# One hybrid decoder layer in float32: attention over memory by products made once from weights and memory

## The chip, the cores and the metric

The kernel runs on one core of a Trainium2 chip. The metric is the device time of one execution in microseconds (us). Of the core's engines PE (TensorE) multiplies matrices, ACT (ScalarE) and DVE (VectorE) do elementwise work, POOL (GpSimd) does elementwise work in SBUF and issues DMAs, and SP issues DMAs.

## What is computed

A prompt of 2048 tokens and 8 single decode tokens, model width 1024, pass through one layer: a mixer (short convolution and mLSTM), attention over 256 memory rows, and a SwiGLU network. The change is in the attention, four heads of width 256:

```python
def mem_kv(mem, g_mem, w_xkv):
    kk, vv = jnp.split(rmsnorm(mem, g_mem) @ w_xkv, 2, axis=-1)
    return kk.reshape(B, M, X_HEADS, X_HEAD_DIM), vv.reshape(B, M, X_HEADS, X_HEAD_DIM)

def cross_attn(xn, mk, mv, w_xq, w_xo):
    q = (xn @ w_xq).reshape(B, T, X_HEADS, X_HEAD_DIM)
    s = jnp.einsum('bthd,bmhd->bhtm', q, mk.astype(q.dtype)).astype(jnp.float32) * (X_HEAD_DIM ** -0.5)
    p = jax.nn.softmax(s, axis=-1).astype(xn.dtype)
    o = jnp.einsum('bhtm,bmhd->bthd', p, mv.astype(xn.dtype)).reshape(B, T, X_HEADS * X_HEAD_DIM)
    return o @ w_xo
```

The prompt has one memory (keys and values from `mem_kv`, both outputs too). Each decode token has its own cached keys and values.

## The kernel before

**Tiling.** Activations lie with features on the partitions and tokens along the rows. The prompt is cut in five blocks of 4, 3, 3, 3 and 3 chunks of 128 tokens (`BLK`). The 8 decode tokens ride as extra columns: in the mixer of block 1 (`DM`), the output and query products of block 2 (`DO`), the attention output and network of block 3 (`DX`).

**Products in three passes.** A float32 product with a weight is made from a rounded high part and a remainder: high by high, high by low, low by high (`gemm`, L518). A weight group is one 128 by 1024 piece (512 KB); a `gemm` of a group is 8 x 3 = 24 matmuls whose moving width is the block's token count (512, 384, or 392 with the decode tokens).

**Weight stream.** The 16 groups of memory weights, then 121 groups per block: gates, sigmoids, four heads of six, output (`O_OUT`, 8), queries (`O_XQ`, 8), attention output (`O_XO`, 8) and network. For the memory groups and block 0, SP loads raw weights into two buffers (`w_raw`, L326), ACT casts the high part into one of `NS` = 5 slots (`w_high`, L823), and DVE (memory groups, L1175) or POOL (block 0, L419) subtracts to get the low part. The subtract frees the raw buffer. In block 0 SP also stores both parts to `split_d` (1 MB); blocks 1 to 4 load them from there, one 1 MB load a group.

**Attention of a block.** Eight query groups with the scores (L682, three-pass, 256 wide), the turning of probabilities (`ptrans`, L692) and the products with the values (`pv`, L699, plain float32) hooked between them; the softmax is `maxima` (DVE, L1439), `exps` (ACT, L1011, 128 by 256 each) and `normalise` (DVE, L1450). Then eight `O_XO` groups.

**Opening.** The kernel makes keys and values of the memory (16 groups, 256 wide), turns the values (L552) and prepares the first block's activations on DVE (L1164, L1170) and ACT (L840).

**Order.** Every engine runs its own program in order, written out by hand; engines meet at semaphores. In `w_high(g)` ACT waits for the raw load of group g + `NS` and for group g to be used up.

**End.** After the last group come the last sum of squares (L526), a root, eight multiplications (L1224), four stores of `y` and three of states.

## Time and profile before

| | |
|---|---|
| runs, median of 3 | 2973.12 us (2971.23 to 2975.67) |
| the profiled execution | 2972.26 us |
| its span, first to last instruction | 2970.5 us |
| PE busy / weight loads | 2921.0 us (98%) / 2759.7 us (93%) |
| DVE / ACT / POOL busy | 1212.2 / 761.0 / 379.7 us |
| moved by DMA | 776.02 MB, 261 GB/s |

The profile is of one execution. A busy engine is one with an instruction in flight; matmuls overlap in their pipeline (a 384-wide one is shown with some 338 ns), so what a matmul costs is read from the chain of waits, whose pieces give a stretch's length and its number of matmuls. A plain float32 product shows as two matmul records.

### The profile page before, as it was taken

How to read it: one execution, taken by the hardware profiler on the slowest of the kernel's cores; microseconds unless marked ns; L12 is line 12 of the kernel's file. 1: busy time of each engine (PE TensorE's matmuls, PEld its weight loads, DVE VectorE, ACT ScalarE, POOL GpSimd, SP SyncE). 2: the span in 40 equal slices, each digit the busy share in tenths (PEclk: the TensorE clock that was granted, in tenths of full speed). 3: DMA queues.
4: the chain of work that ended last, by engine and by line, in shares of the span. 5: the costliest groups of instructions: out<-in, count | busy, mean ns of one | idle time of the engine just before them, and what ended most of it. 6: DMA issues, size and time to landing. Idle time of an engine off the chain costs nothing.

```text
span 2970.5 us, 39232 instructions
## 1 busy us (share of the span) xinstructions
PE 2921.0 (98%) x16162; PEld 2759.7 (93%) x16162; DVE 1212.2 (41%) x2337; ACT 761.0 (26%) x1510; POOL 379.7 (13%) x252
## 2 busy tenths in 40 slices
PE   7899999999999999999999999999999999999998
PEld 6788778888899999999999999999999999999998
DVE  6455554224624444233344546334422243442223
ACT  4443443232332220113232011322311032231001
POOL 0443434444210000000000111000000000000000
PEclk9999999999999999999999999999999999999999
DMA  5876858788876488777667989866467777646675
GB/s 190 321 269 225 282 203 298 277 277 309 300 274 244 162 324 305 264 264 285 219 226 273 338 321 372 308 226 249 174 241 260 260 268 266 229 179 248 254 268 195
DMA packets 126585, 776.02 MB, mean 261 GB/s; under 512 B 14885, under 2 KB 18405, under 8 KB 46665
## 3 DMA queue, kind: packets, MB, share of 16 engines
q1 hardware_dynamic: 109744, 710.71, 66.0%
q0 software_dynamic: 13904, 59.48, 5.8%
q10 hardware_dynamic: 2760, 3.33, 0.4%
q8 instruction: 129, 2.11, 0.3%
q14 instruction: 48, 0.39, 0.0%
HBM read 633.52 MB, written 139.94 MB: 260 GB/s over the span
## 4 chain that ended last, share of the span: by engine, by line
PE 90%; DMA 4%; DVE 2%; ACT 2%; POOL 1%; issue 1%; SPq 0%; DVEq 0%; ACTq 0%
PE gb L518 83%; DMA w_raw<-w_st 2%; PE ta L682 2%; DMA w_hl<-split_d 1%; POOL w_hl L419 1%; PE td L699 1%; PE tb L699 1%; ACT w_hl L823 1%; DMA w_raw<-w_kv 1%; PE ta L603 0%; PE tb L572 0%; DVE w_hl L1175 0%; PE ta L526 0%; PE tb L614 0%; PE td L621 0%
## 5 line engine op out<-in xcount | busy, mean ns | idle before, releaser
L518 PE MATMUL gb<-xn_hi,w_hl 128*128 128x384 f32 (+2 forms) x6440 | 1770.4, 350 | 14.2 <-DVE xn_lo L1170 7.7
L518 PEld LDWEIGHTS gb<-xn_hi,w_hl 128*128 128x128 f32 x6440 | 1178.7, 188 | 73.2 <-DVE xn_lo L1170 8.8
L518 PE MATMUL gb<-xn_lo,w_hl 128*128 128x384 f32 (+2 forms) x3240 | 1123.1, 347 | 0.0
L518 PE MATMUL gb<-act_hi,w_hl 128*128 128x384 f32 (+3 forms) x3296 | 872.4, 344 | 18.4 <-DVE w_hl L1175 10.6
L518 PEld LDWEIGHTS gb<-act_hi,w_hl 128*128 128x128 f32 x3296 | 598.8, 189 | 46.3 <-DVE w_hl L1175 10.9
L518 PEld LDWEIGHTS gb<-xn_lo,w_hl 128*128 128x128 f32 x3240 | 609.5, 188 | 28.7 <-issue 1.2
L518 PE MATMUL gb<-act_lo,w_hl 128*128 128x384 f32 (+3 forms) x1648 | 563.9, 342 | 0.0
L1218 DVE TENSOR_TENSOR work<-gb,r_res 128x384 f32<-128x384 f32 (+2 forms) x260 | 151.8, 585 | 652.0 <-PE gb L518 588.1
L419 POOL TENSOR_TENSOR w_hl<-w_raw,w_hl 128x1024 fp32r<-128x1024 f32 x120 | 292.4, 2440 | 413.7 <-ACT w_hl L823 413.7
L518 PEld LDWEIGHTS gb<-act_lo,w_hl 128*128 128x128 f32 x1648 | 311.6, 189 | 13.6 <-issue 0.7
L1410 DVE TENSOR_TENSOR x<-x,gb 128x384 f32<-128x384 f32 (+2 forms) x200 | 115.4, 581 | 373.2 <-PE gb L518 369.9
L823 ACT ACTIVATE w_hl<-w_raw 128x1024 fp32r<-128x1024 f32 x132 | 138.9, 1057 | 329.6 <-DMA w_raw<-w_st 158.4
L1080 ACT ACTIVATE work<-work 128x384 f32<-128x384 f32 (+2 forms) x110 | 59.9, 545 | 504.1 <-DVE work L1218 504.0
L1083 ACT ACTIVATE act_hi<-work 128x384 fp32r<-128x384 f32 (+2 forms) x110 | 60.1, 546 | 346.2 <-DVE work L1637 346.2
L997 ACT ACTIVATE work<-x 128x384 f32<-128x384 f32 (+2 forms) x120 | 65.6, 546 | 270.0 <-DVE x L1410 249.7
L1420 DVE TENSOR_TENSOR r_res<-r_res,work 128x384 f32<-128x384 f32 (+2 forms) x120 | 94.5, 787 | 68.6 <-ACT work L997 67.2
L1637 DVE TENSOR_TENSOR work<-work 128x384 f32<-128x384 f32 (+2 forms) x110 | 87.4, 794 | 35.2 <-ACT work L1080 24.0
L382 POOL DMA_DIRECT2D big<-rows_d x20 | 10.9, 550 | 675.1 <-DMA rows_d<-big 675.1
L887 ACT ACTIVATE big<-gb,cst 128x384 f32<-128x384 f32 (+1 forms) x80 | 48.5, 607 | 186.6 <-PE gb L518 186.0
L1320 DVE TENSOR_TENSOR work<-ta,big 128x128 f32<-128x128 f32 x64 | 18.7, 292 | 186.8 <-ACT work L968 144.4
L1624 DVE TENSOR_TENSOR act_lo<-work,act_hi 128x384 fp32r<-128x384 f32 (+2 forms) x110 | 85.6, 778 | 12.5 <-ACT act_hi L1083 11.8
L1423 DVE SCALAR_TENSOR_TENSOR xn_lo<-x,cst,xn_hi 128x384 fp32r<-128x384 f32 (+2 forms) x80 | 55.8, 698 | 0.0
(248 smaller groups left out, 1806.9 us busy)
## 6 DMA issues: line engine op xcount, KB each, us to landing
w_hl<-split_d SPq DMA_DIRECT2D x484, 1024.0 KB, 5.2
split_d<-w_hl SPq DMA_DIRECT2D x121, 1024.0 KB, 5.0
w_raw<-w_st SPq DMA_DIRECT2D x121, 512.0 KB, 6.0
w_raw<-w_kv SPq DMA_DIRECT2D x16, 512.0 KB, 3.6
big<-kd_d POOLq DMA_DIRECT2D x8, 1024.0 KB, 9.0
big<-vd_d POOLq DMA_DIRECT2D x8, 1024.0 KB, 11.3
x<-x_blk POOLq DMA_DIRECT2D x8, 768.0 KB, 8.0
big<-x_blk POOLq DMA_DIRECT2D x6, 768.0 KB, 6.0
```

The costliest lines, as they stand in the source:

```text
L419: pool.tensor_tensor(lo_w, raw_w, hi_w.bitcast(F32), ALU.subtract).then_inc(w_lo_done, 1)
L518: mm = pe.matmul(gb[:, ps, 0:wd], a[:, s, k * P:(k + 1) * P], r[:, k, 0:wd], start=(first and k == ks[0] and i == 0), stop=(last and k == ...
L682: mm = pe.matmul(ta[:, t // 2, (t % 2) * 256:(t % 2) * 256 + 256], a[:, kt, t * P:(t + 1) * P], r[:, kt, :], start=(dt == 0 and i == 0), s ...
L823: act.activation(w_hi[:, n % NS, :], w_raw[:, n % NR, :], ACT.Copy).then_inc(w_hi_done, 1)
L997: act.activation(sq_res[:, 0:wd], x[:, e, 0:wd], ACT.Square).then_inc(res_sq, 1)
L1080: act.activation(et[:, 0:W], gt[:, 0:W], ACT.Silu).then_inc(e_ffn, 1)
L1083: act.activation(act_hi[:, f, 0:W], ht[:, 0:W], ACT.Copy).then_inc(hid_hi, 1)
L1218: return lambda ps: v.tensor_tensor(dst[:, 0:wd], ps[:, 0:wd], r_res[:, 0:wd], ALU.mult)
L1410: return lambda ps: v.tensor_tensor(x[:, e, 0:wd], x[:, e, 0:wd], ps[:, 0:wd], ALU.add)
L1420: v.tensor_tensor(acc_res[:, 0:wd], acc_res[:, 0:wd], sq_res[:, 0:wd], ALU.add).then_inc(res_acc, 1)
L1624: v.tensor_tensor(act_lo[:, f, 0:W], ht[:, 0:W], act_hi[:, f, 0:W].bitcast(F32), ALU.subtract).then_inc(hid_lo, 1)
L1637: v.tensor_tensor(ht[:, 0:W], et[:, 0:W], ut[:, 0:W], ALU.mult).then_inc(h_ffn, 1)
```

## The change

Products with two fixed factors are made once: for each head the query weights times the keys (1024 by 256), and the values times the output weights (256 by 1024). Together they are sixteen 128 by 1024 pieces.

- **Opening.** 16 more weight groups follow the memory groups (`w_xq` transposed, `w_xo`), through the same two raw buffers, cast by ACT, subtracted by POOL. From them PE makes 32 banks of product (16 of 12 matmuls 256 wide, 16 of 6 matmuls 512 wide). ACT copies the even banks, DVE the odd; ACT stores all, whole float32, to `made_d` in rows of 1 KB (first 16) and 512 bytes. SP loads them in block 0 as raw weights in the places of queries and attention output. `NS` goes from 5 to 6; the slots take the place of `mem_k_hi`, `mem_k_lo` and `mem_v`.
- **Attention.** `wide(p, ...)` gives the scores of two heads at once: activations are stationary, the made piece moves 512 wide. Two halves, each 24 matmuls for every chunk. Query groups, scores against keys and products with values are gone; the turned probabilities go in three passes straight into `O_XO`. The row sums come as columns (`sum_cols`, one product a chunk).
- **Decode tokens.** Their queries are made apart in block 2 (`decode_queries`, plain float32, 16 products 512 wide, between `O_XO` groups), their attention output in block 3 (`decode_outputs`, 16 such, between `O_OUT` groups, then 8 small turning products). 16 loads of 512 KB on POOL's queue bring the weights.
- **Rows.** In each block three row tiles are now stacked and turned by one product a chunk (12 wide) where there were three (4 wide); their store is two DMAs.
- **Decode pieces.** `PIECE_AT` puts two of them later in block 2's network.
- **End.** The last sum of squares takes its last term as a second product instead of a DVE addition, the table load is earlier, POOL multiplies two of the eight tiles of `y`, and the stores go in the order 0, 2, 6, 4.

```diff
+G_KV = 32
+NPRE = 32
 O_GATE = 0
...
-NS = 5
+NS = 6
...
-PIECE_AT = [2 * f + 1 for f in range(1, 8)] + [16 + m for m in (0, 1, 2, 4, 5, 6)] + [G1 + 2 * f + 1 for f in range(3)]
+PIECE_AT = [2 * f + 1 for f in range(3, 8)] + [16 + m for m in range(8)] + [G1 + 2 * f + 1 for f in range(3)]
...
+def attends(g):
+    return g >= G_KV and O_XQ <= (g - G_KV) % G_BLK < O_FF[0]
...
+                if attends(g):
+                    src = made_d[g - gw(0, O_XQ)]
...
+                    if raws[i] == gw(0, O_XQ):
+                        for slot_stored in pre_stored:
+                            sp.wait_ge(slot_stored, 16 * (NPRE // 8))
...
+            for k in (0, 2, 6, 4):
+                if k == KT - 2:
+                    sp.wait_ge(y_pool, 2)
+                else:
...
+            pool.wait_ge(r_done, r_res_at(NB - 1, 2))
+            for k in (KT - 2, KT - 1):
+                pool.tensor_tensor(x[:, k, 0:W], x[:, k, 0:W], r_res[:, 0:W], ALU.mult).then_inc(y_pool, 1)
...
+            for h in range(HEADS):
+                pe.wait_ge(mem_lo, 2 * h + 2)
+                for j in range(4):
+                    i = h * 4 + j
+                    bank = pre_bank(i)
+                    for n in range(2):
+                        for dt in range(2):
+                            g = G_MEM + 2 * h + dt
+                            if j == 0 and n == 0:
+                                slot_ready(g)
+                            c = (2 * j + n) * P
+                            for f, (a, r) in enumerate([(w_hi, act_hi), (w_hi, act_lo), (w_lo, act_hi)]):
+                                mm = pe.matmul(bank[:, n * NMEM:(n + 1) * NMEM], a[:, g % NS, c:c + P], r[:, 2 * h + dt, NMEM:2 * NMEM],
+                                               start=(dt == 0 and f == 0), stop=(dt == 1 and f == 2))
...
+                for j in range(4):
...
+                    for dt in range(2):
+                        g = G_MEM + KT + 2 * h + dt
+                        if j == 0:
+                            slot_ready(g)
+                        for f, (a, r) in enumerate([(act_hi, w_hi), (act_lo, w_hi), (act_hi, w_lo)]):
+                            mm = pe.matmul(bank, a[:, 2 * h + dt, mt * P:(mt + 1) * P], r[:, g % NS, half * 512:half * 512 + 512],
+                                           start=(dt == 0 and f == 0), stop=(dt == 1 and f == 2))
...
+                def turn_rows():
+                    pe.wait_ge(rows_exp, b + 1)
+                    pick = ident[0:3 * ROWS, 0:3 * ROWS].rearrange("p (i c) -> p i c", c=ROWS)[:, :, 0:HEADS]
                     for c in range(CH):
-                        a = (i * CH + c) * HEADS
-                        mm = pe.matmul(tb[:, a:a + HEADS], row[:, c * P:(c + 1) * P], ident[0:ROWS, 0:HEADS], start=True, stop=True)
...
+                        pe.wait_ge(dw_loaded[i % 4], 16 * ((KT + i) // 4) + 16)
+                        for half, bank in enumerate((ta[:, 1, :], td)):
+                            mm = pe.matmul(bank[0:NDEC, :], dy[:, i * NDEC:(i + 1) * NDEC], dwt[:, i % 4, half * 512:half * 512 + 512],
+                                           start=i == 0, stop=i == KT - 1)
+                        mm.then_inc(dw_used, 1)
...
+                def sum_cols():
+                    pe.wait_ge(res_acc, b * 27 + 9)
                     for t in range(CH):
-                        for dt in range(2):
-                            kt = 2 * h + dt
...
+                def score_bank(p, t):
+                    if p == 0:
+                        return gb[:, (gw(b, O_XQ) + t) % NP, :] if t < NP else gm[:, :]
+                    return (ta[:, 0, :], ta[:, 1, :], td[:, :], tb[:, :])[t]
+                def ptrans(h, mt):
+                    bank = gm if b == 0 and h < 2 else (gm, tb)[mt]
+                    pe.wait_ge(p_done, ch0(b, h // 2 * 2 + 2))
...
+                def wide(p, hooks):
+                    for q in range(4):
+                        g = gw(b, O_XQ) + 4 * p + q
+                        slot_ready(g)
                         for t in range(CH):
-                            m = pe.transpose(bank[:, t * P:(t + 1) * P], prob[:, t, mt * P:(mt + 1) * P], ident)
-                        m.then_inc(pt_done, 1)
-                def pv(h):
-                    pe.wait_ge(pt_evac, (b * HEADS + h) * 2 + 2)
-                    for dt, bank in enumerate((td, tb)):
-                        for mt in range(MT):
-                            mm = pe.matmul(bank[:, 0:TOK], mem_v[:, mt, h * 256 + dt * P:h * 256 + (dt + 1) * P],
-                                           prob_t[:, mt, 0:TOK], start=(mt == 0), stop=(mt == MT - 1))
-                        mm.then_inc(pv_done, 1)
-                opening(gw(b, O_XQ), W, 0)
-                q_hooks = {3: {3: lambda: scores(0)}, 4: {6: lambda: ptrans(0)}, 5: {2: lambda: scores(1) or pv(0)},
-                           6: {6: lambda: ptrans(1) or scores(2)}, 7: {3: lambda: pv(1)}}
-                for m in range(2, KT):
-                    gemm(gw(b, O_XQ + m), W, xn_hi, xn_lo, hooks=q_hooks.get(m))
+                            if q == 0 and p == 0 and t < NP:
+                                read_out(pe, gw(b, O_OUT + KT - NP) + t)
+                            if q == 0 and p == 1 and t == 2:
+                                pe.wait_ge(rcol_done, b + 1)
+                            for n in range(2):
+                                kt = 2 * q + n
+                                if p == 0 and t == 0:
+                                    pe.wait_ge(res_lo, b * 16 + kt + 1)
+                                for f, (a, r) in enumerate([(xn_hi, w_hi), (xn_lo, w_hi), (xn_hi, w_lo)]):
+                                    mm = pe.matmul(score_bank(p, t), a[:, kt, t * P:(t + 1) * P], r[:, g % NS, n * 512:n * 512 + 512],
+                                                   start=(kt == 0 and f == 0), stop=(kt == KT - 1 and f == 2))
+                            if t == CH - 1:
+                                mm.then_inc(group_done, 1)
+                            elif q == 3:
+                                mm.then_inc(s_done, 1)
+                            if (q, t) in hooks:
+                                hooks[q, t]()
+                wide(0, {(1, CH - 1): sum_cols})
+                if b == 0:
+                    wide(1, {(1, 3): lambda: ptrans(0, 0), (2, 1): lambda: ptrans(0, 1), (2, 3): lambda: ptrans(1, 0),
+                             (3, 1): lambda: ptrans(1, 1)})
+                else:
+                    wide(1, {(1, 2): lambda: ptrans(0, 0) or ptrans(0, 1), (2, 2): lambda: ptrans(1, 0) or ptrans(1, 1)})
                 def o_wait(k):
                     pe.wait_ge(o_lo, b * 8 + k + 1)
-                    if b == DX and k == 0:
...
+                def decode_product(i, rows, lhs, bank):
+                    pe.wait_ge(dw_loaded[i % 4], 16 * (i // 4) + 16)
+                    for half in range(2):
+                        mm = pe.matmul(bank[half][0:NDEC, :], lhs, dwt[:, i % 4, half * 512:half * 512 + 512],
+                                       start=rows == 0, stop=rows == KT - 1)
+                    mm.then_inc(dw_used, 1)
...
+            W = w_ffn(NB - 1)
+            pe.wait_ge(res_acc, (NB - 1) * 27 + 26)
+            pe.matmul(ta[:, 0, 0:W], ones, acc_res[:, 0:W], start=True, stop=False)
+            pe.wait_ge(res_sq, NB * 24)
+            pe.matmul(ta[:, 0, 0:W], ones, sq_res[:, 0:W], start=False, stop=True).then_inc(ssq_done, 1)
...
+                pre_left(act, i)
+                h, j = (i // 4) % HEADS, i % 4
+                if i < NPRE // 2:
+                    dst = made_d[4 * (h // 2) + j].rearrange("p (n h m) -> p n h m", n=2, h=2)[:, :, h % 2, :]
+                    src = made[:, i % 8, :].rearrange("p (n m) -> p n m", n=2)
+                else:
+                    kt, m0 = 2 * h + j // 2, KT + j % 2 * 4
+                    dst = made_d[m0:m0 + 4, :, kt * P:(kt + 1) * P].rearrange("m p c -> p m c")
+                    src = made[:, i % 8, :].rearrange("p (m c) -> p m c", m=4)
+                act.dma_start(dst, src).then_inc(pre_stored[i % 8], 16)
+            for i in range(NPRE):
+                if i % 2 == 0:
+                    pre_made(act, i)
+                    after(act, pre_stored[i % 8], 16 * (i // 8))
+                    act.activation(made[:, i % 8, :], gb[:, (G_MEM + i) % NP, :], ACT.Copy).then_inc(pre_a, 1)
+                if i:
+                    store_made(i - 1)
+                if i % 4 == 3:
+                    w_high(G_MEM + i // 4 * 2)
+                    w_high(G_MEM + i // 4 * 2 + 1)
+                if i < KT:
+                    read_out(act, G_MEM - 1)
+                    act.activation(act_hi[:, i, 0:NMEM], vfeat[:, i, :], ACT.Copy).then_inc(mem_hi, 1)
+                elif i < 2 * KT:
+                    next_high(0, i - KT)
+            store_made(NPRE - 1)
...
+                w_high(gw(b, O_XQ))
+                norm_cols(b, r_res_at(b, 0))
+                for q in range(1, 4):
+                    w_high(gw(b, O_XQ + q))
                 exps(0)
-                q_high(3)
-                pt(0)
-                q_high(4)
+                w_high(gw(b, O_XQ + 4))
+                w_high(gw(b, O_XQ + 5))
+                prob_high(0)
+                w_high(gw(b, O_XQ + 6))
+                prob_high(1)
+                w_high(gw(b, O_XQ + 7))
```

ACT at the end of the opening, before: a cast of weights a group, beside casts of activations and keys.

```order
L823 ACTIVATE w_hl<-w_raw 128x1024
L840 ACTIVATE xn_hi<-big 128x512
L873 ACTIVATE mem_k_hi<-x 128x256 x2
L823 ACTIVATE w_hl<-w_raw 128x1024
L873 ACTIVATE mem_k_hi<-x 128x256 x2
L892 ACTIVATE big<-gb,cst 128x512
L823 ACTIVATE w_hl<-w_raw 128x1024
```


ACT after, in the second half of the made products: a copy of a bank, two stores, and after each four banks two casts.

```order
L1083 ACTIVATE big<-gb 128x512
L1077 DMA made_d<-big 128x4x128 x2
L998 ACTIVATE w_hl<-w_raw 128x1024 x2
L1083 ACTIVATE big<-gb 128x512
L1077 DMA made_d<-big 128x4x128 x2
L1083 ACTIVATE big<-gb 128x512
L1077 DMA made_d<-big 128x4x128 x2
L998 ACTIVATE w_hl<-w_raw 128x1024 x2
L1083 ACTIVATE big<-gb 128x512
L1077 DMA made_d<-big 128x4x128 x2
L1083 ACTIVATE big<-gb 128x512
L1077 DMA made_d<-big 128x4x128 x2
L998 ACTIVATE w_hl<-w_raw 128x1024 x2
```


The casts now stand between the copies that free PE's banks. PE in the attention of block 1 before: a query group with two products of values hooked in (`td`, `tb`, 384 wide).

```order
L518 MATMUL gb<-xn_hi,w_hl 128x384 x2
L518 MATMUL gb<-xn_lo,w_hl 128x384
L518 MATMUL gb<-xn_hi,w_hl 128x384
L699 MATMUL td<-big,mem_v 128x384 x2
L699 MATMUL tb<-big,mem_v 128x384 x2
L518 MATMUL gb<-xn_hi,w_hl 128x384
L518 MATMUL gb<-xn_lo,w_hl 128x384
L518 MATMUL gb<-xn_hi,w_hl 128x384 x2
L518 MATMUL gb<-xn_lo,w_hl 128x384
```


PE after in block 1, the second half of the scores: the turning of head 0's probabilities (`gm`, `tb`) between two pieces.

```order
L853 MATMUL td<-w_hl,xn_hi 128x512 x2
L853 MATMUL td<-w_hl,xn_lo 128x512
L853 MATMUL td<-w_hl,xn_hi 128x512
L835 MATMUL gm<-mats,work 128x128 x3
L835 MATMUL tb<-mats,work 128x128 x3
L853 MATMUL ta<-w_hl,xn_hi 128x512
L853 MATMUL ta<-w_hl,xn_lo 128x512
L853 MATMUL ta<-w_hl,xn_hi 128x512 x2
```


The value products have no counterpart. PE in block 2, fifth `O_XO` group, before: one turning of decode queries.

```order
L518 MATMUL gb<-act_hi,w_hl 128x384 x2
L518 MATMUL gb<-act_lo,w_hl 128x384
L518 MATMUL gb<-act_hi,w_hl 128x384
L722 MATMUL tb<-mats,dec 64x128
L518 MATMUL gb<-act_hi,w_hl 128x384
L518 MATMUL gb<-act_lo,w_hl 128x384
```


PE after, in the fourth `O_XO` group: four float32 products for the decode queries (8 rows out, 512 wide); three more such hooks follow.

```order
L613 MATMUL gb<-act_lo,w_hl 128x384
L613 MATMUL gb<-act_hi,w_hl 128x384
L881 MATMUL ta<-dwt,dec 8x512
L881 MATMUL td<-dwt,dec 8x512
L881 MATMUL ta<-dwt,dec 8x512
L881 MATMUL td<-dwt,dec 8x512
L613 MATMUL gb<-act_hi,w_hl 128x384
L613 MATMUL gb<-act_lo,w_hl 128x384
```


One turning is gone, sixteen products have come.

## Rows read from the trace of the kernel before

**Rows 1.** The page, parts 1 and 2: whole kernel.

```profile
PE 2921.0 (98%) x16162; PEld 2759.7 (93%) x16162; DVE 1212.2 (41%) x2337; ACT 761.0 (26%) x1510; POOL 379.7 (13%) x252
...
PEclk9999999999999999999999999999999999999999
```

**Rows 2.** The longest of the waits of PE: us in total, times, longest.

```profile
PE gb L518 <- DVE w_hl L1175: 10.6, 2, 9.4
```

**Rows 3.** Chain of waits, opening of the kernel: start us, us, what.

```profile
26.92 2.88 PE gb L518 x24
...
48.07 3.95 DMA w_raw<-w_kv
...
94.65 5.47 PE gb L518 x24
...
114.45 0.98 PE tb L572 x8
```

**Rows 4.** Chain of waits, attention of block 1.

```profile
985.76 2.15 PE ta L682 x18
...
993.63 0.33 PE gm L692 x3
...
998.54 1.29 PE td L699 x4
...
1015.35 4.16 PE gb L518 x24
```

**Rows 5.** Chain of waits, attention of block 2.

```profile
1553.41 4.22 PE gb L518 x24
```

**Rows 6.** Chain of waits, attention of block 0.

```profile
331.24 4.30 DVE act_lo L1465
...
354.71 1.72 PE td L699 x4
```

**Rows 7.** Groups by form, PE: what, count, busy us, mean ns.

```profile
L682 PE MATMUL ta<-mem_k_hi,act_hi 128*128 128x256 f32 x128 | 37.0, 289 | 1.7 <-DVE act_lo L1465 1.7
...
L699 PE MATMUL td<-big,mem_v 128*128 128x384 f32 x64 | 23.3, 485 | 0.0
```

**Rows 8.** Groups by form, ACT, whole kernel.

```profile
L1011 ACT ACTIVATE work<-ta,work 128x256 f32<-128x256 f32 x64 | 29.5, 469 | 45.6 <-DVE work L1442 45.6
...
L1011 ACT ACTIVATION_READ_ACCUMULATOR work<-ta,work 128x1 f32 x64 | 12.7, 199 | 0.0
```

**Rows 9.** Groups by form, DVE, whole kernel.

```profile
L1450 DVE TENSOR_SCALAR work<-work 128x256 f32<-128x256 f32 x64 | 22.6, 354 | 2.3
...
L1439 DVE TENSOR_REDUCE work<-ta 128x2 f32<-128x512 f32 x24 | 16.6, 691 | 27.8 <-PE ta L682 27.7
```

**Rows 10.** Timeline of ACT, end of the memory stage.

```profile
59.12 1.04 ACT L823 ACTIVATE w_hl<-w_raw 128x1024 fp32r<-128x1024 f32 x1
...
62.65 1.04 ACT L823 ACTIVATE w_hl<-w_raw 128x1024 fp32r<-128x1024 f32 x1
```

**Rows 11.** Timeline of POOL, first subtracts of weights.

```profile
78.44 2.35 POOL L419 TENSOR_TENSOR w_hl<-w_raw,w_hl 128x1024 fp32r<-128x1024 f32 x1 [4.57 <-ACT w_hl L823]
82.15 2.46 POOL L419 TENSOR_TENSOR w_hl<-w_raw,w_hl 128x1024 fp32r<-128x1024 f32 x1 [1.36 <-ACT w_hl L823]
88.05 2.38 POOL L419 TENSOR_TENSOR w_hl<-w_raw,w_hl 128x1024 fp32r<-128x1024 f32 x1 [3.44 <-ACT w_hl L823]
```

**Rows 12.** Timeline of DVE in the same stretch.

```profile
67.13 0.68 DVE L1170 TENSOR_TENSOR xn_lo<-big,xn_hi 128x512 fp32r<-128x512 f32 x1
...
82.33 2.83 DVE L1170 TENSOR_TENSOR xn_lo<-big,xn_hi 128x512 fp32r<-128x512 f32 x1
```

**Rows 13.** The line that loads raw weights: issue to landing, all its loads.

```profile
DMA to landing us min/median/max: 3.1/5.9/11.8
```

**Rows 14.** Chain of waits, last microseconds.

```profile
2959.00 0.57 DVE r_res L1420
...
2962.88 3.17 DVE x L1224 x6
```

572 lines of the change are left out of this document (320 added, 252 removed).

## Prediction

> **What bounds the kernel now.** I read the page first, then the waits of PE, then the chain of waits. PE is busy 98% of the span, and its granted clock stays at the upper level of 2.4 GHz in nearly every slice [rows 1]. The longest of PE's waits sum to 10.6 us, for DVE's weight parts in the opening [rows 2]. From block 1 on the chain is PE, matmul after matmul, and no other engine's work stands in it for long. So a matmul taken away there is worth its spacing, and the opening has to be looked at by itself, since weights and not matmuls set its pace.
>
> The profile shows some 340 ns for one matmul, but they overlap. The cost is a piece of the chain divided by its count: 256 wide 2.88/24 = 0.120 us [rows 3], 384 wide 4.16/24 = 0.173 [rows 4], 392 wide 4.22/24 = 0.176 [rows 5], 512 wide 5.47/24 = 0.228 [rows 3]. A plain float32 product is two records: 384 wide 1.29/2 = 0.645 [rows 4], 512 wide 1.72/2 = 0.86 [rows 6], and a 4-wide turning of a row 0.98/4 = 0.245 [rows 3]. A turning by transpose is 0.33/3 = 0.11 [rows 4].
>
> **PE's work outside the opening.** All of it is on the path.
> - Scores: 24 matmuls a chunk, 16 chunks, 384 x 0.120 = 46.1 us go (a third of them is the first line of [rows 7]).
> - Products with values: 16 a block. 64 x 0.645 + 16 x 0.86 = 55.1 go (the 64 records of `td`, 384 wide, are half of the four narrower blocks [rows 7]).
> - Query groups: 576 x 0.173 + 192 x 0.176 + 192 x 0.228 = 177.2 go; `wide` has 48 matmuls a chunk, 768 x 0.228 = 175.1 come. The columns are the same, only fewer and wider: -2.1.
> - Turning of values, 16 x 0.11: -1.8. Rows: 48 products become 16, 32 x 0.245: -7.8. Eight columns less in `O_XO` of block 3: -0.6.
> - Sums as columns: 17 products of 0.245 for five of some 0.68: +0.8. No row shows one moving column; the 4-wide one is the nearest, and its bounds (nothing to double) are worth 4 us each way.
> - Decode tokens: 32 x 0.86 + 8 x 0.245 = +29.5. No row has a product with 8 rows out; I take the 512-wide price, since its rows with 128 out stream the same columns. The bounds are 0.228 (one pass) and 0.86, so this can be up to 20 us less.
>
> Sum: -46.1 - 55.1 - 2.1 - 1.8 - 7.8 - 0.6 + 0.8 + 29.5 = **-83.2 us**.
>
> Beside the rows on 512-wide matmuls stands a figure of the Trainium skill (TensorE: Matmul & The Clock Gate, "Back-to-back issue gap"): about 131 ns each at 512 columns. By it the scores would come out 768 x 0.097 = 74 us lower still, an estimate. The 24 matmuls of this kernel that took 5.47 us [rows 3] are of the same width and type, so I go by them.
>
> **The opening.** The made products are 192 x 0.120 + 96 x 0.228 = 44.9 us of PE, but their weights come slower. A raw buffer's round is load, cast, subtract. The load is 3.95 in the memory stage [rows 3], with a median of 5.9 over the kernel and up to 11.8 [rows 13]; I take 4.2, near the first, since the stores beside it are 256 KB and not 1 MB. With the cast 1.04 [rows 10], the subtract 2.4 [rows 11] and 0.1 of semaphores it is 7.8 us for one of two buffers, 3.9 a group. The casts of two groups lie 3.5 apart in the memory stage [rows 10], the subtracts beginning at 78.44 and 88.05 are two groups apart, 4.8 each [rows 11]: these are the bounds.
>
> Two things add to 3.9. DVE's operations with two inputs in SBUF stand still beside POOL's subtract: the same one took 0.68 us at 67.13 and 2.83 at 82.33, just as POOL ran 82.15 to 84.61 [rows 11, 12], and in block 0 one of 0.69 took 4.30 [rows 6]. The opening has 24 of these, and they hold POOL likewise. And ACT is in order: after every four banks it casts two groups, six ahead, and while it waits for their load it copies no bank, so PE stops after three. I take 4.4 a group.
>
> The last bank waits for a copy that stands behind the cast of group 35. Group 16's load lands at about 62 (casts of earlier groups at 59.12 and 62.65 [rows 10], one slot more now). 19 groups x 4.4 = 84 brings group 35 to 146; cast 1.1, copy 0.6, last product 1.4, some semaphores: 150. The gate product, 16 x 0.228 = 3.6, ends at 153.5. Before, the piece of 24 at 94.65 [rows 3] holds the last three matmuls of the first sigmoid group (one turning stands after its first 21): that group ended at 95.3 and would have begun, without gaps, at 95.3 - 5.5 - 0.4 = 89.4. So the opening costs **+64 us** with its 44.9 of matmuls; at 3.5 a group +47, at 4.8 +72. Afterwards weights are no nearer to the edge than now: 24 x 0.228 = 5.5 us of PE a group against 4.8.
>
> **Waits in the attention.** In block 1 the first half's softmax has half of the second half, 12 x 3 x 0.228 = 8.2 us, as cover. The second half's last bank is done as the half ends. Then come maximum 0.69 + 0.27, two exponentials with their accumulator reads 2 x (0.47 + 0.20) = 1.34 [rows 8], and reciprocal and two scalings 0.16 + 2 x 0.35 [rows 9]. Behind the two earlier banks that is 4.1 us. PE has four pieces of `O_XO`, 4 x 6 x 0.173 = 4.2. It just fits. In block 0 a cast stands ahead of the exponentials, and four banks take some 7.5 us against 5.5: 2 us. That one replaces some of block 0's stall before the scores, where DVE took 4.30 [rows 6]. The decode weights are loaded 13 us ahead of their use (two groups of 4.2 and three float32 pairs), longer than the longest raw load [rows 13]. I put all new waits less the old ones at **+2 us** (range -3 to +20).
>
> **The end.** An addition of 0.57 leaves the path [rows 14]. DVE multiplies six tiles (3.2 us as the six of [rows 14]) and not eight; POOL's two, by size 0.9 each from its 2.4 a group [rows 11], either run beside them (-1.1) or in turn with them (+0.7), since they have two inputs in SBUF on both sides [rows 12]. **-0.3 us**.
> The Trainium skill (SBUF — State Buffer, "Who interferes with whom") has it that such a pair excludes one another for the whole instruction; by that rule, to which [rows 12] agrees with 2.83 against 0.68, the end would come to +0.1, without it to -1.7.
>
> **Sum.** -83.2 + 64 + 2 - 0.3 = -17.5. From the profiled execution's 2972.26 that is 2954.8; its median of runs lies 0.9 higher, so 2955.6, say **2955 us**.
>
> **Rivals.**
> 1. *The stream is smooth.* Loads keep the memory stage's 3.5 us a group [rows 10], since PE, ACT and DVE have little else: -17. 2938. For it: stores are small. Against: the subtract on POOL is twice as long as DVE's was.
> 2. *The softmax comes late.* If maximum, exponentials and scaling go one after another, three banks take 3 x 3.2 = 9.6 from 2.7 before the half's end, 6.9 against 4.2 of cover, and the second turning waits for its evacuation too: about 4 us a block, 20 in all. 2975, no change. It decides from 4.2 us after the half. For it: only 0.1 us of slack by rows.
> 3. *The stores of made products slow the stream; slower than before.* 32 stores go out in rows of 512 bytes and 1 KB beside the loads. If a load then takes 8.4, inside the 11.8 seen [rows 13], a group takes 6.0, and 19 x 6.0 puts the gate's end at 183: +93. 2985. It decides at 5.5 us a group, a load of 7.3. Against: 4.8 is what 1 MB stores did to it [rows 11].
> 4. *A 512-wide matmul in `wide` is spaced like a 256-wide one.* 768 x (0.228 - 0.120) = 83 less: 2872. Against it stand the 24 in 5.47 [rows 3].
> The Trainium skill's figure, above, points this way and gives 2881 as an estimate.
> 5. *The change does not do what it says*: the columns of queries and of new scores are equal, so if the values' and scores' time had been hidden, nothing is gained. But those pieces stand in the chain itself [rows 4]; I give it nothing of its own.
>
> **Chances.** Forecast (2944 to 2966) 0.58; rival 1 0.14, the cheap decode products with it 0.03; rival 2 0.12; rival 3 0.10; rival 4 0.01; something else 0.02. For 8 in 10 the range goes from 2936, with most of rival 1 in it, to 2972, without rival 3 and the upper part of rival 2. A measurement of this kernel tells a change from none at about 0.2%, 6 us. Faster by more than that is the forecast, rivals 1 and 4 and a quarter of rival 2: 0.80; within it 0.10; slower 0.10.
>
> **What the profile after would show.** The gate product's end near 153, and waits of PE in the opening put down to ACT's copies and POOL's subtracts; casts 4.4 us apart on average from group 16 on. `O_XQ` of block 1 as 144 matmuls in 33 us with no wait inside, and the attention of blocks 1 to 4 each some 19 us shorter (72 x 0.120 + 16 x 0.645 + 0.4). The decode products at 0.86 each. I am wrong if the opening's end is off by more than 10 us, if PE waits before the turning of heads 2 and 3 in every block, or if PE loses time in block 2's network to the later decode pieces.

## Result: slower by 0.4%

The changed kernel takes 2982.5 us (median of 6), the kernel before 2970.9 beside it (median of 6); the ratio is 1.0037, 95% interval 1.0025 to 1.0049. The forecast was 2955, faster. One of the six executions of the changed kernel took 3214 us at a granted clock of 0.85; the ratio leaves it out, and the median of the other five is 2982.1. Its profiled execution took 2980.44 us, with a span of 2978.6.

The page, parts 1 and 4 (chain: share of the span by engine), which answer to [rows 1]:

```profile
PE 2892.0 (97%) x15739; PEld 2706.0 (91%) x15739; DVE 1177.9 (40%) x2240; ACT 754.5 (25%) x1472; POOL 427.9 (14%) x286
...
PE 85%; DMA 6%; DVE 2%; POOL 2%; ACT 2%; issue 2%; SPq 0%; ACTq 0%; DVEq 0%
```

PE's busy time fell by 29 us, and the time still rose: PE stands still more. Where, is seen when the first matmul of each stage is looked up in both traces (us from the start of the span; the last row ends with the execution). "Forecast" is made of the prediction's own terms.

| stage | before | after | change | forecast |
|---|---|---|---|---|
| up to the end of the gate product | 89.4 (without gaps) | 159.7 | +70.3 | +64 |
| block 0, rest of the mixer | 182.1 | 191.6 | +9.5 | -3.8 |
| block 0, mixer's output products | 44.0 | 44.0 | 0 | 0 |
| block 0, attention and `O_XO` | 119.2 | 104.7 | -14.5 | -23.2 |
| block 0, network | 362.0 | 361.8 | -0.2 | 0 |
| blocks 1 to 4 and the end | 2175.6 | 2118.7 | -57.0 | -54.5 |

From block 1 on all came as forecast and 2.5 us better. Everything that is missing, 28 us, is missing before block 1 begins: at 861.8 instead of 796.6 us, +65 where +37 was forecast.

The longest waits of PE in the first 505 us (us in total, times, longest), which answer to [rows 2]:

```profile
PE gb L613 <- DVE w_hl L1396: 11.2, 2, 9.2
PE gb L678 <- ACT big L1083: 10.6, 3, 7.2
PE gb L613 <- DVE act_lo L1371: 9.1, 4, 4.2
PE gb L660 <- issue: 6.6, 3, 3.5
PE tb L733 <- DVE work L1550: 6.4, 4, 2.7
PE gb L853 <- DVE x L1639: 5.8, 2, 4.6
PE tb L697 <- ACT work L1137: 4.9, 1, 4.9
```

The first of them stood in the kernel before too, with 10.6 us [rows 2]. The others are put down to DVE, to ACT and to nothing that the profile shows ("issue"), none to POOL, at many places in the program. That scatter suggests one cause behind them. The chain of waits points at it; here it is at the end of the opening (start us, us, what):

```profile
129.12 1.06 ACT w_hl L998
...
130.26 2.37 POOL w_hl L482
132.65 4.88 DMA w_raw<-w_st
...
137.55 1.07 ACT w_hl L998
...
138.69 2.40 POOL w_hl L482
141.11 0.33 SPq L391
...
141.48 9.05 DMA w_raw<-w_st
...
150.56 1.06 ACT w_hl L998
...
151.69 2.38 POOL w_hl L482
...
154.45 8.23 DMA w_raw<-w_st
```

It is the round of one raw buffer, load, cast, subtract, next load, with no PE in it: 13.0 us from the load at 141.48 to the one at 154.45, for every second group, so 6.5 us a group. It goes on like this past 178 us, with a load of 11.55 at 166.63. PE uses up a group in 5.5 where nothing stands between its matmuls.

What stood in the attention of block 1 [rows 4] is gone, and its successor has no wait in it (chain; the sum columns are the second line):

```profile
1033.53 8.20 PE gb L853 x36
1041.73 0.56 PE td L817 x6
1042.29 8.31 PE gb L853 x36
1050.61 2.72 PE ta L853 x12
...
1058.77 0.33 PE gm L835 x3
```

### The profile page after: what moved, and what is told of

It is laid out like the page before. It is cut to its first block, busy times and chain, and to the rows that moved or that the text cites. A ratio compares the mean times of both kernels' runs of the same rounds, so it can differ in the third digit from the quotient of the medians.

```text
span 2978.6 us, 38344 instructions
## 1 busy us (share of the span) xinstructions
PE 2892.0 (97%) x15739; PEld 2706.0 (91%) x15739; DVE 1177.9 (40%) x2240; ACT 754.5 (25%) x1472; POOL 427.9 (14%) x286
## 2 busy tenths in 40 slices
DMA packets 143974, 801.14 MB, mean 269 GB/s; under 512 B 15949, under 2 KB 31693, under 8 KB 64057
## 4 chain that ended last, share of the span: by engine, by line
PE 85%; DMA 6%; DVE 2%; POOL 2%; ACT 2%; issue 2%; SPq 0%; ACTq 0%; DVEq 0%
PE gb L613 75%; DMA w_raw<-w_st 3%; PE gb L853 3%; POOL w_hl L482 2%; PE ta L853 2%; DMA w_raw<-w_kv 2%; ACT w_hl L998 1%; PE td L853 1%; DMA big<-kd_d 1%; DMA w_raw<-made_d 0%; PE ta L722 0%; PE gm L835 0%; DVE work L1550 0%; PE tb L733 0%; DVE w_hl L1396 0%
## 5 line engine op out<-in xcount | busy, mean ns | idle before, releaser
L613 PE MATMUL gb<-xn_hi,w_hl 128*128 128x384 f32 (+2 forms) x5800 | 1582.8, 349 | 4.4 <-DVE x L1639 1.4
L613 PEld LDWEIGHTS gb<-xn_hi,w_hl 128*128 128x128 f32 x5800 | 1061.0, 188 | 53.2 <-issue 5.3
L613 PE MATMUL gb<-xn_lo,w_hl 128*128 128x384 f32 (+2 forms) x2920 | 1011.9, 347 | 0.0
L613 PE MATMUL gb<-act_hi,w_hl 128*128 128x384 f32 (+3 forms) x3296 | 872.1, 344 | 22.2 <-DVE w_hl L1396 11.2
L613 PEld LDWEIGHTS gb<-act_hi,w_hl 128*128 128x128 f32 x3296 | 599.5, 189 | 55.9 <-DVE w_hl L1396 11.5
L613 PEld LDWEIGHTS gb<-xn_lo,w_hl 128*128 128x128 f32 x2920 | 548.9, 188 | 24.2 <-issue 0.5
L482 POOL TENSOR_TENSOR w_hl<-w_raw,w_hl 128x1024 fp32r<-128x1024 f32 x136 | 330.2, 2433 | 495.2 <-ACT w_hl L998 495.2
L1447 DVE TENSOR_TENSOR work<-gb,r_res 128x384 f32<-128x384 f32 (+2 forms) x220 | 128.3, 585 | 555.4 <-PE gb L613 522.0
L998 ACT ACTIVATE w_hl<-w_raw 128x1024 fp32r<-128x1024 f32 x147 | 154.6, 1057 | 390.9 <-DMA w_raw<-w_st 157.5
L853 PE MATMUL gb<-w_hl,xn_hi 128*128 128x512 f32 x240 | 78.0, 397 | 5.8 <-DVE x L1639 5.8
```

The source lines that it names most:

```text
L482: pool.tensor_tensor(lo_w, raw_w, hi_w.bitcast(F32), ALU.subtract).then_inc(w_lo_done, 1)
L613: mm = pe.matmul(gb[:, ps, 0:wd], a[:, s, k * P:(k + 1) * P], r[:, k, 0:wd], start=(first and k == ks[0] and i == 0), stop=(last and k == ...
L853: mm = pe.matmul(score_bank(p, t), a[:, kt, t * P:(t + 1) * P], r[:, g % NS, n * 512:n * 512 + 512], start=(kt == 0 and f == 0), stop=(kt ...
L998: act.activation(w_hi[:, n % NS, :], w_raw[:, i % NR, :], ACT.Copy).then_inc(w_hi_done, 1)
L1447: return lambda ps: v.tensor_tensor(dst[:, 0:wd], ps[:, 0:wd], r_res[:, 0:wd], ALU.mult)
```

## The experiments

**Theory S**: up to block 1 the stream of raw weights is late, because a load can only be issued when its buffer has gone through cast and subtract, and there are two buffers. Rivals: the order of work on ACT's queue (Q); the bytes themselves, made products' stores above all (B); POOL's subtract, by its length or by what it does to DVE (P). Each run's ratio is to the kernel before on the same chip, with its 95% interval; "block 1 at" is the start of its first matmul in the trace. To compare: changed kernel 2982.5, block 1 at 861.8.

**ACT's order.** The casts of groups 34 and 35, `w_high(28)` and `w_high(29)`, go behind the last score bank's copy on ACT:

```
-                if i % 4 == 3:
-                    w_high(G_MEM + i // 4 * 2)
-                    w_high(G_MEM + i // 4 * 2 + 1)
+                if i % 4 == 3 and i != 27 or i == 30:
+                    w_high(G_MEM + i // 4 * 2 - 2 * (i == 30))
+                    w_high(G_MEM + i // 4 * 2 + 1 - 2 * (i == 30))
```

> The changed kernel, with ScalarE's casts of groups 34 and 35 behind its copy of the last score bank instead of ahead of its last two copies. There the last bank waited 7.2 us. Theory Q (the order on ScalarE is what costs the opening): the gate product ends 6 to 7 us earlier and all of it is kept, 2975 us. Theory S (the stream of raw weights, load and cast and subtract through two raw buffers, is late up to the end of block 0, whoever waits for it): the gate product ends earlier, but the sigmoid and head groups of block 0 wait for their weights by as much more, block 1 begins within 2 us of 862, 2980 us.

Measured: 2983.4, ratio 1.0038 (1.0023 to 1.0053), block 1 at 864.2. The gate product began at 148.6 instead of 156.1, and PE lost all of it again before block 1. That is what theory S expected, and Q falls. The 7.2 us wait was the largest single one in the new code, and taking it away was worth nothing here.

**The stores of made products taken away**, with their waits:

```
-                act.dma_start(dst, src).then_inc(pre_stored[i % 8], 16)
```

> The changed kernel without the 32 stores of made products (8 MB) and without the waits for them; attention loads its own weights from where the products would not have been stored, so its result means nothing there. Same loads, casts, subtracts, matmuls and copies. Theory S1 (these stores lengthen the raw loads beside them): the raw loads that took 8 to 11.5 us at 141 to 178 us take 5 to 6, block 0's waits (rows at 185, groups at 208 and 214) go, and the time falls by 15 to 25 us, to 2955 to 2965. Rival (the loads are long because of the 1 MB stores of split weights and the 2 MB of memory outputs, and the opening is paced by POOL's subtract in the round): less than 4 us, 2977 or more.

Measured: 2975.4, ratio 1.0010 (1.0000 to 1.0019), block 1 at 850.8. The stores cost 7 us by the medians and 11 by the traces (the traced execution, 2969.6, is the fastest of the ten), where the theory had 15 to 25 and its rival under 4. The loads of 117 to 250 us hardly changed: 5.9 us in the median, up to 11.0, against 6.0 and 11.5. So the stores are a part, not the cause.

**Groups 16 to 31 subtracted by DVE** (`w_low`), not POOL:

```
-                if g + NS < G_MEM:
-                    w_low(g + NS)
+                w_low(g + NS)
...
+                if i % 4 == 3:
+                    for n in (G_MEM + NS + i // 4 * 2, G_MEM + NS + i // 4 * 2 + 1):
+                        if n < G_KV:
+                            w_low(n)
```

> The changed kernel with the subtracts of groups 16 to 31 on DVE (0.7 to 1.3 us each), as in the memory stage, instead of POOL (2.4 us). Theory S2 (the round of a raw buffer is load plus cast plus subtract, so a shorter subtract shortens it, by 1.2 to 1.7 us for two groups): 16 groups give 10 to 14 us in the opening, 2967 to 2971 if it is kept. Rival (the transfers limit the opening, as the DMA share above 90% there says): the loads become longer by what the subtract became shorter, within 4 us of the changed kernel. Second rival (DVE, which also copies half of the banks, is now held by late casts): slower, up to 2990.

Measured: 2979.0, ratio 1.0022 (1.0012 to 1.0031), block 1 at 856.8: 3.5 us by the medians and 5 by the traces, under half of the 10 to 14 that the shorter subtract promised. Where the rest went was not taken apart.

**No weights for the made products**: the sixteen groups are neither loaded nor cast nor subtracted.

```
-    return g < G_LOW
+    return g < G_MEM or G_KV <= g < G_LOW
```

> The changed kernel without load, cast and subtract of groups 16 to 31; the made products are computed from whatever weights are in the slots, so the attention's result means nothing. Matmuls, copies and stores of the opening stay. Theory S (weights set the pace of the opening): the 32 banks take their 45 us of matmuls plus few waits, the gate product ends at 125 to 130 instead of 160, and 25 to 35 us are gained, 2945 to 2955. Rival (the copies of the banks, alternately by ScalarE and DVE, and the reuse of the 8 made buffers by their stores set the pace): the gate product ends at 145 or later, 2965 or more.

Measured: 2958.6, ratio 0.9952 (0.9938 to 0.9967), block 1 at 839.1. The score banks now take 23.0 us for 23.0 of matmuls (39.2 in the changed kernel): there the coming of the weights set the pace, nothing else. The gate product ended at 135, 5 us later than I said, and the run gained 24 us where I said 25 to 35; the last bank still waited 7.9 us for its copy on ACT.

**Slots and buffers.** `NS` is the number of weight slots (8 KB a partition each), `NR` that of raw buffers (4 KB). The change raised `NS` from 5 to 6. There is room for 56 KB in all and not for 60, so six slots go with two raw buffers only.

```
-NS = 6
-NR = 2
+NS = 5
+NR = 2, 4 or 3
```

> The changed kernel with five weight slots as before the change instead of six. Theory S: slots do not matter where the raw stream is late (the opening and block 0), so the same within 3 us up to block 1; a sixth slot costs a cast ahead of the first products (start about 5 us later than before the change), which comes back here. 2976 to 2982. Rival (the sixth slot gives the lead that block 0 and the attention need): waits for split weights in blocks 1 to 4 beside the stores, 2985 or more.

> Five weight slots and four raw buffers instead of six and two. With four loads under way the round of a buffer (load 6 to 11 us, cast 1.1, subtract 2.4) no longer limits the stream; only the sum of bytes, ScalarE and POOL do. Theory S-latency (the round through two raw buffers is the limit): opening and block 0 together 20 to 30 us shorter, 2952 to 2962. Rival S-bandwidth (the transfers themselves are at their limit, 8 MB of made products, 16 loads, and 1.5 MB a group in block 0): loads overlap but each takes twice as long, gain under 5 us, 2975 or more. Rival Q: ScalarE's order, then the banks wait for casts as before, gain 5 to 10.

> Five weight slots and three raw buffers: between five and two (2973 us) and five and four (2944 us). Theory S-latency (the round of a raw buffer, divided by their number, limits the stream): a round of some 9.5 us over three buffers is 3.2 a group, already under the 5.5 of PE in block 0 but not always over the memory stage's needs, so three give most of the 29 us, 2946 to 2955. Rival (with four, what helped was something else, as the earlier start of the memory stage alone): half of it or less, 2958 or more.

| `NS`, `NR` | time | ratio (95%) | block 1 at | from there to the end of the span |
|---|---|---|---|---|
| 6, 2 (changed kernel) | 2982.5 | 1.0037 (1.0025 to 1.0049) | 861.8 | 2116.8 |
| 5, 2 | 2973.2 | 1.0007 (0.9998 to 1.0016) | 847.8 | 2124.5 |
| 5, 3 | 2942.2 | 0.9896 (0.9882 to 0.9911) | 817.8 | 2122.7 |
| 5, 4 | 2943.9 | 0.9901 (0.9885 to 0.9918) | 818.8 | 2122.8 |

One more raw buffer, at five slots, is worth 31 us, and a fourth nothing. Between 5, 2 and 5, 3 only the number of buffers changes, so S is shown. All three runs came out faster than their forecasts under S (2976 to 2982, 2952 to 2962, 2946 to 2955). All of the gain comes before block 1: the gate product begins at 129.4 instead of 148.4 us, so 19 of the 30 us lie in the opening, and 11 in block 0. The casts of groups 16 to 35 came 3.9 us apart instead of 4.4. What ended the idle time of ACT ahead of the casts between 160 and 350 us, in the changed kernel (us, times):

```profile
  issue: 29.1, 10
  DMA w_raw<-w_st: 27.9, 8
```

and with five slots and three raw buffers:

```profile
  PE gb L613: 5.8, 1
  DMA w_raw<-w_st: 1.7, 1
  issue: 0.3, 1
```

ACT hardly waits for a load any more. (In the kernel before, with two buffers, its casts waited 18.1 us for loads in the same window.) The loads themselves did not become shorter. The DMA view of 160 to 250 us (changed kernel, then three buffers: issues, KB each, median us to landing):

```profile
DMA packets 6177, 25.45 MB, mean 283 GB/s; under 512 B 581, under 2 KB 2215, under 8 KB 4264
...
w_raw<-w_st SPq DMA_DIRECT2D x13, 512.0 KB, 6.0
```

```profile
DMA packets 5158, 26.70 MB, mean 297 GB/s; under 512 B 572, under 2 KB 572, under 8 KB 3232
...
w_raw<-w_st SPq DMA_DIRECT2D x16, 512.0 KB, 7.0
```

Each load took longer, 7.0 us, and more of them were done. The whole kernel moves the same 801.14 MB with two, three and four buffers, so the 31 us are not a matter of bytes (B) but of how many loads were under way. The two windows do not hold the same work: the memory outputs lie inside the first and ahead of the second.

The sixth slot is a bad trade for this: it costs 14 us ahead of block 1 and gives 8 back later. I had expected the same time within 3 us up to block 1. Of the 14, 6.7 are there when the first made product begins (77.9 instead of 71.1 us: a sixth load, cast and subtract stand ahead of it); how the rest arises was not taken apart. Of the 8, 5.5 lie in the last of the three parts of block 2's network, where the decode pieces move data (63.8 us with five slots, 58.2 with six).

**The kernel before with four raw buffers and four slots**, the only such pair for which it has room:

> The kernel before the change with four raw buffers and four weight slots, instead of two and five (it has no room for more). Theory: before the change the stream was late only up to the first sigmoid group (some 12 us of waits there), so four raw buffers give at most that, and four slots lose it again beside the decode stages: 2965 to 2985. Rival (the buffers' gain has nothing to do with the change and would come to the kernel before alike): 2945 or less.

Measured: 2974.9, ratio 1.0012 (1.0002 to 1.0021). Block 1 began at 783.1 instead of 796.6, and four slots lost 14 us again after that. So block 1 can come 13 us earlier in the kernel before too, and the 31 us do not come to it. How much of the 13 is the buffers' doing is not shown, for this run also has a slot less: the gate product began 7.9 us earlier (67.1 instead of 74.9), and in the changed kernel a slot less alone brought the first made product 6.7 us forward. Between these two runs with more buffers block 1 differs by 817.8 - 783.1 = 34.7 us. That is near the +37 of the forecast, but the forecast was for two buffers, so the agreement is luck.

**The memory outputs moved**: with two raw buffers from group 38 to group 24, as below, and with four to group 44 (`off == 12`):

```
-                if off == 6:
+                if off == -8:
...
-                    if G_KV <= raws[i]:
+                    if G_MEM <= raws[i]:
```

> The changed kernel with the two 1 MB stores of memory keys and values issued beside raw group 24 (in the middle of the opening) instead of group 38, where raw loads took 8 to 11.5 us and the rows' stage waited for ScalarE. Theory S-bandwidth: the bytes are moved, not taken away, and the opening is as full: the same within 3 us, 2980. Rival (there is room among the transfers of the opening, none at 160 to 180): 4 to 6 us less, 2975.

> Four raw buffers, and the two 1 MB outputs of memory keys and values issued beside group 44 instead of 38. With four raw buffers ScalarE waited 14.9 us for the last stores of made products, whose last took 22 us beside these two outputs, and PE 11.4 us for ScalarE. Theory B (transfers in each other's way; bytes at the wrong place): that wait falls to under 5 us, 6 to 9 us gained, 2935 to 2938. Rival (the last stores are slow by themselves, in rows of 512 bytes): under 2 us, 2943.

Measured: 2980.6 with two buffers, ratio 1.0026 (1.0016 to 1.0036), block 1 at 861.4: what block 0 won, 4 us, the opening lost. With four buffers and the late place 2941.5, ratio 0.9901 (0.9886 to 0.9916), block 1 at 817.6 instead of 818.8. The first is as its theory had it, bytes moved and nothing won. In the second its theory fell: it gained 2.4 us by the medians, the last stores of made products still took 20 to 25 us without these neighbours, and PE waited 6.2 us for ACT where the view of waits has 11.2 for the run before it.

**What the opening still loses with enough buffers.** With three, the longest waits of PE in the first 505 us are these; in the second, ACT itself waits for the last store (chain, second fence):

```profile
PE gb L613 <- DVE w_hl L1396: 11.2, 2, 9.4
PE gb L613 <- ACT big L1108: 8.2, 1, 8.2
```

```profile
136.63 20.23 DMA made_d<-big
```

ACT waits for all 32 stores ahead of the first sigmoid tile, though only that tile's own place has to be free. Without stores (four buffers), and with the waits given out by slot (three buffers):

```
-                if b == 0:
-                    for slot_stored in pre_stored:
-                        act.wait_ge(slot_stored, 16 * (NPRE // 8))
                 for h in range(HEADS):
+                    if b == 0:
+                        for slot_stored in (pre_stored[0:1], pre_stored[1:2], pre_stored[2:3], pre_stored[3:8])[h]:
+                            act.wait_ge(slot_stored, 16 * (NPRE // 8))
```

> Four raw buffers, without the 32 stores of made products and without the waits for them (attention reads other weights of the same size, so its result means nothing). With two raw buffers the stores cost 11 us. Theory B: with the round no longer in the way, what the opening still loses is the stores' doing, the 11.4 us wait ahead of the sigmoid groups above all: 2928 to 2933. Rival (the rest of the opening's waits are of casts, subtracts and copies in turn on ScalarE and DVE): 2938 or more.

> Five weight slots, three raw buffers (2942 us), and ScalarE waits for the stores of made products by slot: for slots 0 to 2 ahead of the sigmoid tiles that lie over them, for the other five only ahead of the rows' store, not for all eight ahead of the first sigmoid tile. Theory B (the 8.4 us wait of PE at 149 us is that wait for the last stores): it goes, 6 to 9 us less, 2933 to 2936. Rival (the rows' stage needs the last stores just as soon, or the sigmoid groups then wait for their weights): under 3 us, 2940.

Measured: without stores 2933.5, ratio 0.9873 (0.9856 to 0.9889), block 1 at 808.4, so 10 us, and half a us above what the theory had. By slot 2940.6, ratio 0.9895 (0.9880 to 0.9910), block 1 at 812.9, 5 us less than with three buffers alone. But the traced execution, 2936.0, is the fastest of its four, and the medians are only 1.6 apart. PE's 8.2 us became 5.1 ahead of the rows' turning, since the rows need the last slots. By the medians the rival holds; that half of the theory came true is seen in the one trace alone.

**Three small parts on top of that run**: the subtracts of groups 16 to 31 on DVE; the casts of groups 34 and 35 later, as in the first experiment, with the memory outputs at group 44; and the last output's eight tiles all on DVE:

```
-                    for k in range(KT if bb < NB - 1 else KT - 2):
+                    for k in range(KT):
```

> As e12, and the subtracts of groups 16 to 31 on DVE instead of POOL. In the opening's chain DVE's two-input operations stand for 2.4 to 2.9 us where they took 0.3 to 0.7 beside no subtract of POOL. Theory P (DVE and POOL hold each other): without POOL's subtracts these take 0.3 to 0.7 again, the first score banks (gaps of 3.7, 1.8 and 3.0 us) come without waits, 4 to 8 us less than e12. Rival (DVE's added 16 subtracts of 0.7 to 1.3 take its time instead, and its copies of banks come later): within 2 us of e12 or slower.

> As e12, with the casts of groups 34 and 35 behind the last score bank's copy (as in e1, which gave nothing with two raw buffers) and the two outputs of memory keys and values at group 44. Theory S (e1's earlier gate product was lost again because the stream was late): now that the stream has slack, what the last banks wait for ScalarE's casts, about 2 us of PE, is kept: 1 to 3 us less than e12. Rival (no effect beyond the runs' scatter): within 1 us of e12.

> As e12, with all eight tiles of the last output scaled by DVE, none by POOL, in the order 0 to 7. In the changed kernel DVE's three tiles beside POOL's two took 1.35 us each instead of 0.60, and from the last matmul of the network to the end it took 16.0 us instead of 14.8. Theory P: that comes back, less the 0.57 us of the removed addition: 14.3 us from that matmul to the end, 1 to 2 us less than e12. Rival (the last stores to memory set the end, whoever scales): 16 us as before.

Measured, in this order: 2937.4 (ratio 0.9885, 0.9870 to 0.9900), 2944.1 (0.9908, 0.9894 to 0.9923) and 2938.5 (0.9888, 0.9872 to 0.9905). Executions of one and the same kernel lie up to 7 us apart here, so differences of a few us between medians of four say little, and the traces have to speak. In the first, PE's waits of 3.6 and 2.8 us in and after the score banks became 1.7 and 0.6, and others of 2.2 and 1.5 came. The gate product begins 1.4 us earlier, but block 1 begins at 814.4 where the run without it has 812.9: a gain of 4 to 8 us is not shown. The second is slower, by a new wait of PE of 10.0 us for ACT at 172 us. The later memory outputs brought it: DVE waited 24.1 us for the second of them, and ACT for DVE. Whether ACT's order alone is worth anything there stays open. In the third the time from the start of the network's last matmul to the end of the span is 12.6 us, against 14.0 in the run without it: 1.4 us, within its theory.

**All together**, without the later casts and memory outputs:

> Three raw buffers and five slots, waits for the made products' stores by slot (e12), subtracts of groups 16 to 31 on DVE (e13), the last eight tiles all on DVE (e15). By the traces: block 1 begins at 811 to 815 us instead of 862 (e12 813, e13 814), blocks 1 to 4 as in the runs with five slots (2108 us to the last matmul's start), and from there 13 us instead of 14: 2933 to 2938. If e13's and e15's parts do nothing, it stays with e12's 2940.

Measured: 2936.5 us, ratio 0.9882 (0.9866 to 0.9899), block 1 at 812.0, as expected. That is 1.2% faster than the kernel before and 46 us faster than the changed kernel; 31 of them are the raw buffer, 9 the slot given up for it.

## Why the prediction was wrong

**PE's work: right.** The price of each piece from the chain before carried over. A wide matmul is 8.20/36 = 0.228, as taken from 24 of the opening [rows 3], and not 0.131. (In the sum, 64 x 0.645 + 16 x 0.86 is 55.0 and not 55.1.) Blocks 1 and 4 gave 19.4 us of attention each, as said. A decode product was taken at 0.86 with bounds down to 0.228; it is 0.86, and 0.95 for the first of each four (chain of block 2; the third line is the sixteen records of the turning of eight rows):

```profile
1600.29 0.95 PE ta L881 x2
1601.25 0.86 PE td L881 x2
...
2096.27 1.88 PE tb L794 x16
```

The sum columns took 0.56/3 = 0.19 each and not 0.245. From block 1 on mixers became shorter by 2.2 us a block and not 1.5; what the other 0.7 are was not tried.

**Waits in the attention, rival 2: right from block 1 on.** The softmax fits; PE has no wait ahead of the turnings of heads 2 and 3. In block 0 it waits 3.2 us there, against the 2 forecast.

**The opening's pace with two buffers: right, its start not.** From the cast of group 16 to that of 35 the changed kernel took 150.6 - 66.4 = 84.2 us for 19 groups, 4.43 each; I had 4.4. But group 16's cast began at 66.4 where I had its load land at 62. With five slots the same cast began at 63.6: I had looked at what a sixth slot gives and never at what it costs. The gate product ended at 159.7 instead of 153.5.

**The step that failed** is the last sentence on the opening: "Afterwards weights are no nearer to the edge than now: 24 x 0.228 = 5.5 us of PE a group against 4.8." The 4.8 is half a round with loads near the median of 5.9, read from one pair of subtracts. It was not even the pace of the kernel before: over the first 16 groups of block 0 its casts came 6.1 us apart. The casts of the same groups (32 to 48) came 6.27 us apart in the changed kernel, and 5.63 with three buffers. A round was 13.0 us at the end of the opening, where loads of 8 to 11.5 us stand beside the last made stores, the 1 MB stores of split weights and the memory outputs; such loads stood in [rows 13] as a maximum, and I used them for rival 3 alone.

That step also asked the wrong question. It compared the weights' pace with PE's, and put nothing for what stands behind a cast on ACT outside the opening. With two buffers ACT waits at its casts for a load, in order, and what PE needs next comes after that. The load issued at 182.19 landed at 187.95; then ACT did (timeline of ACT in the changed kernel):

```profile
188.01 1.06 ACT L998 ACTIVATE w_hl<-w_raw 128x1024 fp32r<-128x1024 f32 x1 [4.48 <-issue]
189.09 0.63 ACT L1131 ACTIVATE work<-work 32x512 f32<-32x512 f32 x1
...
190.00 0.63 ACT L1137 ACTIVATE work<-work 32x512 f32<-32x512 f32 x1
```

PE waited 4.9 us for the last of these, which makes the rows ready. Its waits of 2.2 and 2.7 us that end at 210.9 and 217.4 follow casts at 208.0 and 213.7 in the same way. With three buffers PE has no wait over 0.4 us between 158 and 415 us. So the mixer took 9.5 us more instead of 3.8 less, and the attention won 14.5 instead of 23.2; with three buffers the stretch from the start of the gate product to the output products fell from 195.3 to 186.9 us, and the wide products of block 0 from 54.2 to 46.5, which is nearly all of the attention's missing 8.7. Why the kernel before, with two buffers and casts 6.1 us apart, waited less at the same places was not tried.

**Rival 3** gave 2985 and the other sign, near the result. Its mechanism is only a part of it. It wanted 5.5 us a group in the opening, which were 4.4, and the stores are worth 7 to 11 us in all.

**The end: wrong, +1.2 us instead of -0.3.** The chain's last lines answer to [rows 14]:

```profile
2968.15 0.62 DVE x L1454
2968.77 1.26 DVEq L177
2970.03 2.85 DVE x L1454 x4
```

DVE's second tile ends 1.26 us behind its first and not 0.53. The group of POOL's two tiles in that stretch:

```profile
L578 POOL TENSOR_TENSOR x<-x,r_res 128x384 f32<-128x384 f32 x2 | 2.6, 1324 | 476.0 <-ACT r_res L1024 476.0
```

They took 1.32 each, by size I had 0.9, and two of DVE's, the second and the third, took 1.34 to 1.35 beside them instead of 0.60 (two, and not three as I wrote ahead of the run with all eight on DVE). In the trace the two engines take turns: POOL's first ends 0.85 us after DVE's first, DVE's second 0.42 after that, POOL's second 0.85 after that. The rule of the Trainium skill (SBUF — State Buffer, "Who interferes with whom"), that the two exclude each other for a whole instruction, agrees with these rows better than my half price, though it too gave only +0.1. The multiplications are the smaller part of the miss. They came to +0.4 us, less than the 0.6 of the addition that is gone. The larger part is on SP's queue: behind the stores of `y` the issues of the first two state stores take 1.02 and 0.98 us instead of 0.50 and 0.54, and the last issue ends 7.8 us after the root instead of 6.4. With all eight tiles on DVE and the stores of `y` in their old order, both the multiplications and these issues are back at the old values, and the end came to -0.5. Whether POOL's part or the order of the stores made the issues longer is open.

**The signs of being wrong** that the prediction names did not catch it. The gate's end was within 10 us, the turnings of heads 2 and 3 had no wait from block 1 on, and block 2's network took 279.3 us against 281.7 before. No sign looked at PE's waits in block 0.

## To carry to other kernels

The pace of a stream through few buffers is read over the whole stretch that it has to feed, long transfers included, and not from one round near the median. PE waits that are put down to several engines at many places can have such a stream behind them. When a change frees memory, try it first where the chain of waits goes round a buffer (31 us here for 4 KB a partition), and cost a deeper queue also at its start. A wait in new code that is long is not yet a wait that is worth something: the first experiment took 7 us away and nothing was gained.

## What the runs showed of the hardware

Some gaps of PE cost more than their length, since the granted clock was lower behind them. Where PE was busy 16 of 26 us, at the end of the opening, the granted clock was 0.80, and at the start 0.70. It is not so for every gap: with PE busy 7 of 13 us from 77 to 90 it stayed at 1.00 (changed kernel; us; PE, PEld, DVE, ACT and POOL busy; PEclk, DMA share, GB/s):

```profile
20.00:40.00 20.00, 13.18 (x84) 12.30 (x84) 9.95 (x17) 9.74 (x17) 0.00 (x0) 0.70 0.55 195
...
77.00:90.00 13.00, 7.00 (x52) 6.45 (x53) 10.84 (x12) 5.47 (x11) 7.28 (x4) 1.00 0.51 177
...
130.00:156.00 26.00, 16.02 (x54) 11.80 (x54) 3.60 (x6) 8.19 (x12) 12.47 (x6) 0.80 0.96 324
```

The value banks' matmuls show both levels, 1.2 and 2.4 GHz: they begin 0.228 us apart at the upper one and 0.427 at the lower, as behind the 7.2 us wait that ended at 152.15. Of the 96, 25 began further apart than at the upper level without a wait between, and that cost 4.6 us between 117 and 155 us. Two thirds of them as a group (ns, min/median/max of one); the longest began right behind that wait:

```profile
L678 PE MATMUL gb<-w_hl,act_hi x64: 388/389/793, 117.1 to 154.4; 128*128 128x512 f32 x64
```

A 256 KB store written in rows of 512 bytes landed after 20.2 us at the end of the opening with three raw buffers; the first seven such stores, issued between 98 and 110 us, took 2.5 to 4.2.

DVE's operations with two inputs in SBUF became longer beside POOL's subtract, in a chain that shows nothing of POOL. In the changed kernel POOL's ran from 85.09 to 87.51 us and two from 91.85 to 96.76 (changed kernel; then operations of the same shapes in the run where DVE subtracts, start us, us):

```profile
85.35 2.44 DVE act_lo L1421
...
94.54 2.77 DVE big L1385
```

```profile
78.30 0.42 DVE act_lo L1428
78.72 0.66 DVE big L1383
```
